# Sixteen rows of two weight loads issued as small transfers of their own

## The reference, cut to what matters

```python
def moe_ffn(h, w_router, b_router, w_gate_up, b_gate_up, w_down, b_down):
    logits = h @ w_router + b_router
    top_val, top_idx = lax.top_k(logits, TOP_K)          # 4 of 32 experts
    gates = jax.nn.softmax(top_val, axis=-1)
    ...
    gu = xblk @ w_gate_up[e] + b_gate_up[e]              # 1024 x 2048 per expert
    gate, up = gu[:, :D_FF], gu[:, D_FF:]
    gate, up = jnp.minimum(gate, 7.0), jnp.clip(up, -7.0, 7.0)
    glu = gate * jax.nn.sigmoid(1.702 * gate)
    y = ((up + 1.0) * glu) @ w_down[e] + b_down[e]       # 1024 x 1024 per expert
```

## Time and profile before

| | us |
|---|---|
| median of 3 runs | 1220.21 |
| lowest and highest | 1217.98, 1220.80 |
| the profiled execution's own time | 1220.07 |
| its span in the profile | 1218.3 |
| TensorE busy in the span | 1194.6 |
| granted clock, mean share of full speed | 0.998 |

### The profile page before, as it was taken

The page is one execution under the profiler, slowest core; times in us unless marked ns, Lnnn a source line. Parts: engine busy times, 40 slices in busy tenths (PEclk is TensorE's granted clock), DMA queues, the critical chain, the costliest instruction groups (busy, mean ns, idle before and its releaser), DMA issues.

```text
span 1218.3 us, 18292 instructions
## 1 busy us (share of the span) xinstructions
PE 1194.6 (98%) x7828; PEld 576.8 (47%) x7828; DVE 446.8 (37%) x967; ACT 260.2 (21%) x637; POOL 43.3 (4%) x101
## 2 busy tenths in 40 slices
PE   8999999999999999999999999999999999999996
PEld 6776777745344344444443444344443444343332
DVE  3366766754313332332233133223332323222324
ACT  3114534522221111111120211011111111111203
POOL 8000110100000000000000000000000000000000
PEclk9999999999999999999999999999999999999999
DMA  9732202499999999999999999999999999999996
GB/s 286 180 105 70 76 6 72 129 396 389 376 426 428 426 417 425 428 430 431 433 428 430 431 431 431 429 431 431 430 430 430 431 433 429 430 432 429 423 423 227
DMA packets 49388, 436.11 MB, mean 358 GB/s; under 512 B 11525, under 2 KB 26952, under 8 KB 31770
## 3 DMA queue, kind: packets, MB, share of 16 engines
q1 hardware_dynamic: 48180, 431.74, 85.8%
q0 software_dynamic: 960, 3.02, 0.8%
q10 hardware_dynamic: 166, 0.15, 0.0%
HBM read 430.01 MB, written 4.89 MB: 357 GB/s over the span
## 4 chain that ended last, share of the span: by engine, by line
PE 86%; DMA 12%; DVE 1%; issue 0%; ACT 0%; SPq 0%; DVEq 0%
PE bank L1626 31%; PE bank L1664 15%; PE bank L920 10%; PE bank L1592 7%; DMA ring<-in_w_gate_up 7%; PE bank L1698 4%; PE bank L1387 3%; DMA ring<-in_w_down 3%; PE bank L1655 2%; DMA mix<-in_w_gate_up 2%; PE bank L1689 1%; PE bank L1139 1%; PE bank L907 1%; PE bank L953 1%; PE bank L1116 1%; DMA hx<-in_state_shift 0%
## 5 line engine op out<-in xcount | busy, mean ns | idle before, releaser
L1626 PE MATMUL bank<-ring,mix 128*64 128x512 f32 x1504 | 344.0, 598 | 4.3 <-DMA ring<-in_w_gate_up 4.3
L1626 PEld LDWEIGHTS bank<-ring,mix 128*64 128x64 f32 x1504 | 101.6, 136 | 203.1 <-issue 197.8
L1664 PE MATMUL bank<-ring,mix 128*64 128x512 f32 x736 | 168.2, 598 | 1.3 <-DMA ring<-in_w_down 1.3
L2952 DVE TENSOR_TENSOR hTb<-bank,w2a 128x512 f32<-128x512 f32 x32 | 22.1, 691 | 367.9 <-PE bank L1655 367.9
L920 PE MATMUL bank<-hTb,ring 128*128 128x328 f32 (+1 forms) x416 | 122.9, 446 | 0.4 <-issue 0.2
L2200 ACT ACTIVATE mix<-bank,nf 128x256 f32<-128x256 f32 x64 | 26.8, 470 | 448.3 <-PE bank L1592 448.2
L1626 PE MATMUL bank<-mix 128*64 128x512 f32 x500 | 112.8, 595 | 2.6 <-DMA mix<-in_w_gate_up 2.3
L3005 DVE TENSOR_TENSOR mix<-mix,bank 128x512 f32<-128x512 f32 x70 | 48.2, 688 | 162.5 <-PE bank L1698 146.6
L920 PEld LDWEIGHTS bank<-hTb,ring 128*128 128x128 f32 x416 | 77.1, 191 | 33.4 <-issue 2.3
L1664 PEld LDWEIGHTS bank<-ring,mix 128*64 128x64 f32 x736 | 49.4, 136 | 90.5 <-issue 84.6
L1626 PEld LDWEIGHTS bank<-mix 128*64 128x64 f32 x500 | 35.2, 137 | 72.8 <-issue 70.8
(11 more groups left out here) (449 smaller groups left out, 1117.2 us busy)
## 6 DMA issues: line engine op xcount, KB each, us to landing
ring<-in_w_gate_up SPq DMA_DIRECT2D x30, 4096.0 KB, 26.1
ring<-in_w_gate_up SPq DMA_DIRECT2D x32, 2048.0 KB, 18.0
ring<-in_w_down SPq DMA_DIRECT2D x15, 4096.0 KB, 26.6
mix<-in_w_gate_up SPq DMA_DIRECT2D x10, 4096.0 KB, 26.3
ring<-in_w_down SPq DMA_DIRECT2D x14, 2048.0 KB, 17.1
mix<-in_w_gate_up SPq DMA_DIRECT2D x11, 2048.0 KB, 16.8
mix<-in_w_down SPq DMA_DIRECT2D x5, 4096.0 KB, 28.7
ring<-in_w_in SPq DMA_DIRECT2D x14, 1024.0 KB, 5.6
```

Of the source, the lines that this page charges most:

```text
L1626: last_ = mm(b_[64 * half:64 * half + 64, :].rearrange("s (p q) -> s p q", q=4), toks, cols[:, half], start=(c == 0), stop=(c == KT - 1))
L1664: last_ = mm(b_[r:r + 64, :], lhs, w[:, o:o + NCOL], start=(j == 0 and q == 0), stop=(j == 1 and q == 3))
L2952: v.tensor_tensor(halves(gg), halves(banks[3][:, :]), bias(e, 0), ALU.add).then_inc(S("g1"), 1)
```

## The change

Up pieces 0 and 1 of the last expert are no longer loaded in one transfer of 128 rows each. The first 112 rows go in one transfer. The last 16 rows (partitions 112 to 127, 16 KB each) follow: for piece 0 in eight transfers of two rows (32 KB), for piece 1 in two transfers of eight rows (128 KB). All go to the same place in SBUF and to the same semaphore, and `piece_counts()` counts nine and three transfers for the pieces instead of one, so TensorE still waits until a whole piece has landed.

```diff
+UNEVEN = {PLACE["up", NE - 1, 0]: 2, PLACE["up", NE - 1, 1]: 8}
...
-            n[s] += 1
+            n[s] += 1 + (16 // UNEVEN[k] if k in UNEVEN else 0)
             out.append((s, 16 * n[s]))
...
+                elif k in UNEVEN:
+                    src, r = rows_in(kind, e, j), P - 16
+                    load(slot_[0:r, :], src[0:r], f"w{SLOT[k]}_in")
+                    while r < P:
+                        load(slot_[r:r + UNEVEN[k], :], src[r:r + UNEVEN[k]], f"w{SLOT[k]}_in")
+                        r += UNEVEN[k]
                 else:
                     load(slot_, rows_in(kind, e, j), f"w{SLOT[k]}_in")
```

## The result

The changed kernel took 1240.03 us (median of 4 runs, 1238.66 to 1242.89); beside it the kernel before took 1219.10 (4 runs, 1217.70 to 1220.80). The ratio is 1.0171, with a 95% interval from 1.0159 to 1.0183: slower by 20.9 us, where 4.5 were forecast. The profiled execution took 1239.36 us around a span of 1237.5, so its span is 19.2 us longer than that of before.

A forecast was written before the change was run, and what follows sets the result against it. DMA transfers and TensorE were taken to run neck and neck, with almost no slack at the end. Small parts 4.0 + large parts 1.0 - slack 0.5 = +4.5 us on 1220.07, giving 1224.6 us; 8-in-10 range 1218.6 to 1231.0.

The forecast's parts named there:

- the large parts: The 112-row transfers of up pieces 0 and 1, nearly as smooth as 128 rows: +1.0 us, between bounds 0 and 4.6.
- an upper end of 4.6 us: Bound for the 112-row transfers: their 3.67 MB at 0.65 of the rate, as beside b_gate_up's 64-row load.
- The small parts: Transfers of two and eight rows behind the 112: they run badly and hold up others, +4.0 us.
- The slack: TensorE began the last down half 0.50 us after its data landed, so 0.5 us of lateness is absorbed.
- The issues: Ten more transfers issued on SP, 0.32 us each, fit in front of waits for buffers: cost 0.
- Balance: Rival, chance 0.20: small parts run on engines that are ahead, later landings come 1.2 us sooner, 1218.9 us.
- Heavy: Rival, chance 0.12: two loaded engines write at half speed and the large parts slow too, +12.7 us.
- SP's queue was full for longer: Rival, chance 0.01: SP issues down halves so late that engines run dry; costs nothing until SP loses over 20 us.
- Hidden: Rival, chance 0.20: rows more and rows less cancel, last landing stays within 0.5 us of its place, 1220.1 us.
- TensorE's wait for piece 0: Sign: it grows from 0.50 us to some 3 us or more, and a wait for piece 1 appears.
- The rate was below 400: Sign: the DMA rate at 1160 to 1175 us falls below 400 GB/s.
- The down halves: Sign: the last expert's down halves land some 5 us later, at even distance again.

The follow-up runs named there:

- one_of_16: Against the changed kernel, the last 16 rows of both pieces go in one transfer each, still behind 112 rows: 1236.65 us, +17.3 over the kernel before.
- two_of_64: Against the kernel before, the last expert's up pieces 0 and 1 are each loaded as rows 0 to 63 and 64 to 127: 1234.91 us, +15.7.
- rows_96_32: Against the kernel before, the last expert's up pieces 0 and 1 are each loaded as rows 0 to 95 and 96 to 127: 1235.60 us, +16.9.
- eight_of_16_step: Against the kernel before, up pieces 0 and 1 each go in eight transfers of 16 rows that lie eight apart: 1234.23 us, +15.0.
- plus_two_apart: Against the kernel before, eight extra two-row loads behind whole piece 0, rows (0, 4) to (35, 39), to those partitions of a free buffer: 1219.86 us, +0.6.
- plus_sixteen_high: Against the kernel before, rows 112 to 127 are loaded again in one transfer behind whole piece 0, into a free buffer: 1223.66 us, +4.9.
- plus_one_high: Against the kernel before, rows 120 to 127 are loaded again in eight one-row transfers behind whole piece 0, into a free buffer: 1222.26 us, +3.5.

## Why the prediction was wrong

**The step that failed** is the price of the large parts: "112 rows are much nearer to 128 than to 64, so I take 1.0". The cut into blocks of rows was nearly the whole affair. one_of_16, which has the 112 rows and a single transfer for each 16, lost 17.3 of the 20.9 us; its rate is down to 265 GB/s where that of whole pieces with the same 16 rows behind them is 429; and two_of_64 and rows_96_32 lose 15.7 and 16.9 with no load under 32 rows. The number of rows was the wrong scale. A row of the trace was near enough to doubt it: the 64 rows of b_gate_up ran at 279 GB/s, and I let them set an upper end of 4.6 us by scaling the time of the parts' own bytes. That too was too low. The rate was half or less, not 0.65, and it was so for everything in flight, for some 35 us, where the two parts' own bytes are 8.5 us at full rate.

**The mechanism.** What the runs show is that the price hangs on which partitions a transfer writes: two rows a transfer cost 6.2 us at one place and nothing clear of noise at another; the write end decides, not the read end; blocks of 64 rows are slow and alternating rows are not; and a single row written to partitions 120 to 127 took double time together with one other packet. The account that fits all of it is that a transfer in which engines write other partitions than in a load of all 128 rows slows these engines and those whose partitions they are. While pieces of such a shape are among the transfers that the engines work on, the sum is mostly 210 to 223 GB/s, and it hits unchanged pieces too: the wait of 4.95 us is for the piece ahead. The Trainium skill's DMA: Bandwidth & Descriptors, section Back-pressure in remote DMA, says of transfers between cores that a saturated write port clogs the path of the other engines on it. These runs are loads from HBM, so its case is another one, but it fits how the harm spreads. What stays open: no view numbers the engines, so which engine wrote which rows of a 64-row load is inferred from the times alone, and the rival reading named under eight_of_16_step stands; why the sum settles near one half for every cut (112 + 16, 96 + 32, 64 + 64, eight of 16), and why it fell to 144 and 167 GB/s in one window of the changed kernel and of one_of_16, was not found.

**The small parts**, +4.0 on record, had nearly the right size, 3.6 beside the large parts and 6.2 alone, and half of the mechanism. They did run on few engines and hold up others, but not because they have few rows: plus_two_apart has as few and costs +0.6. b_down's loads also write only some partitions, 64 to 95, which may be why their row measured the right thing. That the size came out near is partly luck. **The slack** of 0.5 us was too small to matter. **The issues** cost nothing, as said: the 14 of the changed kernel took 11.96 us where four had taken 11.93.

**A second thing was missed**: TensorE's clock. Waits of 0.5 us left it at 1.00 in every window before; around waits of 4.33 to 6.77 us it fell to 0.50, and 5.4 us of the loss are matmuls at the lower clock. The length of a wait alone does not tell when it falls: it fell with a wait of 2.55 us in plus_sixteen_high and stayed at 1.00 through one of 2.66 us in plus_one_high. Some of the 5.4 us would be waiting at the full clock: a wait for a late landing is shorter by what the matmuls ahead of it took longer. That is argued; no run held the clock up.

**The rivals.** Balance was half right: engines that get eight more rows can very nearly have the lead for it (plus_two_apart), but rows 112 to 127 written by them cost 6.2 us. The sentence of the Trainium skill that I weighed against it, from SBUF — State Buffer, section Door 1: The DMA port swizzle, was the one that pointed at the cause; I applied it to the two engines of the small transfers and not to the 16 of the large ones. Heavy, at +12.7, was nearest and still short. SP's queue was full for longer, 32.73 us for four issues in place of 14.89, 17.8 us more and so under the 20 us from which it was to cost something; it cost nothing. Hidden fell. The range's lower end stands as 1218.6 where the sum for balance gives 1218.9, and nothing hangs on that.

**The signs named in advance.** TensorE's wait for piece 0 grew to 6.77 us and one for piece 1 appeared (4.33), as said for 3 or more. The rate was below 400 from 1160 to 1175, but at 216 to 246, and it had already fallen from 1155. The down halves were not late for TensorE; I had them 5 us late and setting the end. SP's full-queue issues were longer.

**Nothing was gained by any version.** Columns and alternating rows, 0.9997 and 1.0005, are no different from the kernel before, which stays the best.

## What to carry to other kernels

Cut a weight load that has to be cut by columns, or into even and odd rows; both were free, while two blocks of rows cost 15.7 us on 4 MB. Judge a transfer's shape by the partitions that it writes, and as far as is known by which engine writes them, not by how many rows or bytes it has, and look at GB/s beside the DMA share, since the share stayed at 1 while the rate was halved. And when a load shape that the trace hardly shows enters a stream that has no slack, price what it does to everything in flight, neighbours ahead of it included, not only to its own bytes.

## What the runs showed of the hardware

- Loads cut at row 112, 96 or 64, or into rows eight apart, ran near half rate, mostly 210 to 223 GB/s in place of 430, and down to 144 in a window with small transfers among them.
- Cuts by columns and into even and odd rows kept the full rate (433 GB/s in a window of both).
- The contention sits at the write end: 223 or 436 GB/s by destination partitions alone.
- Single-row transfers to partitions 120 to 127 left 390 GB/s in the worst window and still cost 3.5 us: 16 packets took about twice their 0.61 us, and nearly all others kept it.
- Transfers of two and of eight rows ran on two and on eight engines, by the count of packets (32 more in the changed kernel).
- TensorE's granted clock fell to 0.50 around waits of 4.33 to 6.77 us in the changed kernel and with one of 2.55 us in plus_sixteen_high; with waits of 0.5 us, and one of 2.66 us in plus_one_high, it did not move.
